# Value projection of the second mixer in products of 512 columns, its weights read twice

## The chip, the cores and the metric

One core of one Trainium2 chip runs the whole program. The metric is the device time of one execution in microseconds (us); the kernel before is given by the median of three runs.

## What is computed

Two transformer blocks on 512 tokens of width 1024, all in float32. The first block mixes by convolutions, attention and pooling and then has a feed-forward part and a gate; the second block has sliding-window attention with sinks and a gated linear attention (GLA), and then a gated feed-forward part with a short convolution. The part around the change is the second block's mixer:

```python
z = h @ w_in[l]
qa, ka, va, qb, kb, vb, rb, gk_lr, ga, gb = split_cols(z)
...
yb = gla_chunked(qb..., kb..., vb.reshape(B, S, H_B, DV_B), gk...)
yb = rmsnorm(yb, gla_norm_g[l]) * jax.nn.silu(rb...)
```

`vb` is 1024 columns wide (4 heads of 256). GLA sums over tokens, so `vb` is wanted with tokens on the partitions, while the other projections are wanted with features on the partitions.

## The kernel before, in words

The 512 tokens are the free dimension of nearly every tensor; features lie on the 128 partitions in 8 tiles of 128. A weight comes as blocks of 128x128; eight blocks, in the order in which they are used, make a **chunk** of 128x1024 (512 KB), and one list, the plan, holds all 1872 blocks (`NBLK`). Each chunk is loaded by a DMA on SP's queue into one of three raw buffers WR, rounded by ACT to its high half WH (`w_hi`, line 2156), and DVE takes WR minus WH as its low half WL (`w_lo`, line 2561). There are four buffers of WH and WL: the high half of a chunk waits until PE has left the chunk four before it (`w_used`), and `ahead` issues it when PE starts a chunk, three chunks ahead; `rest` issues the low half some blocks later, and with it the next load. Activations are split in the same way (AH, AL), and each product is three matmuls: high times high, low times high, high times low.

The order of the work on all five engines comes from one class, `Order`: it writes down steps with `say`, and each engine's program is the same list of steps, of which it runs its own. Between the products of the main line, `tick` is called; side work (a generator that yields how many ticks to wait) puts its next steps there. So a tick is the unit in which side work is spread over the main line, and an engine's instructions stand in the order of the steps: an instruction that waits holds back all behind it on that engine.

The value projection (`values`, `mm_values`, called by `mixer2` after the four `qb` tiles) has the tokens' activations as the stationary operand (128 tokens) and the weights as the moving one. It goes by four quarters `q` of 256 columns; in each by two halves `p` of the tokens (two token tiles of 128); in each over the 8 feature tiles `kt`, with six matmuls of 256 columns and one tick per `kt`. One PSUM bank holds the two token tiles' 256 columns. The half `p` = 1 uses the same weight blocks as `p` = 0, so 64 blocks (8 chunks) serve all. ACT evicts a half bank per token tile (`vb`, line 2465).

Three pieces of side work run between these products:

- `unit2`, the window attention, 16 units: two score products into PSUM (`scores2`, line 2025, P<-KA,QA), a mask and maximum on DVE (`mask2`, lines 3059, 3065, 3067), exponentials on ACT (`exp2`, lines 2388, 2390), a reciprocal on DVE (`scale2`, lines 3073, 3075) and the scaling on ACT (line 2397, SB<-SB,WST), a transpose on PE (`turn2`, line 2033, P<-C,SB), its copy on ACT (line 2406, PT<-P), and the value product (`values2`, line 2046).
- `levels`, the GLA scores by seven levels: differences of the decays (`lv_ref`: DVE line 3087 and POOL line 3501, EX<-BC), their exponential on ACT (`lv_exp`, line 2419, EX<-EX), the scaled queries on DVE (`lv_scale`, lines 3103, 3106, ST<-G,EX) and keys on POOL (line 3522, KT<-G,EX), the **level products** on PE (`lv_mm`, line 2069, P<-ST,KT), and the **puts** of the result on DVE (`lv_put`, lines 3117 to 3119 and 3126, AT<-P). The scaled queries and keys of a level wait for the level products of the level before, and `lv_ref` of the next level waits for the scaled queries and keys of this one.
- the conversions `w_hi` and `w_lo` of the chunks to come.

PSUM banks 0 to 3 are a ring: `ring` takes the closed one that was closed first, `close` gives one back, and the first matmul into a bank waits for its last reader (`free`).

Of the kernel before, what the change touches and what calls it, by code (L numbers as in the profile page):

```python
# [17 lines left out]
CH = 8  # L18
# [4 lines left out]
NBLK = 1872  # L23
# [140 lines left out]
def block(name, r0, c0, nr=128, nc=128):  # L164
    return ((0, 0, name, r0, nr, c0, nc),)
# [31 lines left out]
class Order:  # L197
# [234 lines left out]
    def values(self, q, name, c0):  # L432

        ids = []
        for p in range(2):
            t = self.ring()
            for kt in range(8):
                if p == 0:
                    ids.append(len(self.plan))
                    self.plan.extend(block(name, kt * 128, c0 + 128 * b) for b in range(2))  # L440
                else:
                    for i in (ids[kt], ids[kt] + 1):
                        self.ahead(i)
# [568 lines left out]
    def mixer2(self, post):  # L1012
# [660 lines left out]
def tensor_program(e, w, order, at, m):  # L1673
# [132 lines left out]
    def mm_values(t, p, i, x, kt):  # L1806
        c, wh, wl, ends = weights(i, 2)
# [3 lines left out]
        if kt == 0:  # L1811
            free(t)
        for n in range(2):
            P = m.bank[t.bank][:, 256 * n:256 * n + 256]
            s = slice(256 * p + 128 * n, 256 * p + 128 * n + 128)
            e.matmul(P, xh[:, s], wh, start=kt == 0 and n == 0, stop=False, skip_group_check=True)  # L1816
            e.matmul(P, xl[:, s], wh, start=False, stop=False, skip_group_check=True)  # L1817
            ins = e.matmul(P, xh[:, s], wl, start=False, stop=kt == 7, skip_group_check=True)  # L1818
        if kt == 7:
            ins.then_inc(*at.up("full", "full", t.id))  # L1820
            if ends and p:
                at.also(("full", t.id), "w_used", c)
        elif ends and p:
            ins.then_inc(*at.up("w_used", "w_used", c))
# [265 lines left out]
    def st_mm(n, q, t):  # L2090
        free(t)
        w.wait_ge(*at("st_kd", n))
        w.wait_ge(*at("vb", 3, 3))
# [7 lines left out]
    def gla_out(hh, eh, t):  # L2101
        free(t)
        w.wait_ge(*at("diag_put", 3))
        w.wait_ge(*at("vb", 3, 3))
# [38 lines left out]
def scalar_program(e, w, order, at, m):  # L2143
# [317 lines left out]
    def vb(q, n, t):  # L2461
        if n % 2 == 0:
            w.wait_ge(*at("full", t.id))
        w.wait_ge(*at("roots", "4"))
        e.activation(m.VB[:, n, 256 * q:256 * q + 256], m.bank[t.bank][:, 256 * (n % 2):256 * (n % 2) + 256], ACT.Copy,
                     scale=m.roots("4", 4)[1][:, n:n + 1]).then_inc(*at.up("vb", "vb", q, n))
        if n % 2 == 1:
            at.also(("vb", q, n), "read", t.id)
# [1202 lines left out]
```

## Time and profile before

| | |
|---|---|
| median of 3 runs | 1427.76 us (1426.56 to 1428.2) |
| the profiled execution | 1427.68 us, of which the span from first to last instruction is 1425.9 us |
| PE busy | 1413.9 us, 99% of the span |
| DVE, ACT, POOL busy | 69%, 45%, 15% of the span |
| the value projection, 706.8 to 790.2 us of the span | 83.4 us: PE 82.96, DVE 63.98, ACT 45.98, POOL 29.61 us busy |
| TensorE's granted clock | 0.998 of full speed over the span |

A matmul's duration in the trace includes its way through the array, so matmuls overlap and their durations don't add up to time. The distance from one start to the next does. Times in the text are counted from the start of the span.

### The profile page before, as it was taken

The page shows a single profiled execution, that of the slowest core. Times are in us where ns is not written, and L with a number is a line of the kernel's source. Part 1 is how long each engine was busy: PE and PEld are TensorE (multiplying, and loading weights), DVE is VectorE, ACT ScalarE, POOL GpSimd, SP SyncE. Part 2 cuts the span into 40 slices and gives each one's busy share as a digit, 9 for nine tenths or more (in the row PEclk, how much of TensorE's full clock was granted, in tenths as well). Part 3 has the DMA queues.
Part 4 walks back from the last instruction along what each step waited for, and adds up shares of the span by engine and source line. Part 5 has one row for each costly group of instructions (what it writes and reads, how often), then busy time and mean ns, then how long its engine had stood idle before and what let it go on. Part 6 is the DMA issues. An engine that isn't in the chain of part 4 may idle for free.

```text
span 1425.9 us, 20562 instructions
## 1 busy us (share of the span) xinstructions
PE 1413.9 (99%) x8054; PEld 1213.9 (85%) x8054; DVE 986.4 (69%) x1537; ACT 647.0 (45%) x1028; POOL 214.8 (15%) x136
## 2 busy tenths in 40 slices
PE   9999999999999999999999999999999999999998
PEld 6776798889989888887799888888888889999997
DVE  5777477876676657897696736534452888888877
ACT  5345535534345434545464546323332545455450
POOL 4175224000000011330052104000021000000000
PEclk9999999999999999999999999999999999999999
DMA  6222212333233332222211211323323233333331
GB/s 242 89 75 69 65 60 89 100 97 115 93 100 104 119 104 74 89 67 82 74 60 41 65 45 59 110 90 101 98 90 92 87 105 103 103 93 116 104 106 73
DMA packets 36352, 130.00 MB, mean 91 GB/s; under 512 B 4040, under 2 KB 4296, under 8 KB 36256
## 3 DMA queue, kind: packets, MB, share of 16 engines
q1 hardware_dynamic: 35968, 128.44, 28.5%
q8 instruction: 64, 1.05, 0.3%
q14 instruction: 32, 0.26, 0.1%
q10 hardware_dynamic: 288, 0.26, 0.1%
HBM read 126.56 MB, written 2.10 MB: 90 GB/s over the span
## 4 chain that ended last, share of the span: by engine, by line
PE 91%; DVE 5%; ACT 2%; issue 1%; DMA 1%; ACTq 0%; DVEq 0%; SPq 0%
PE P L1728 17%; PE P L1730 16%; PE P L1729 16%; PE P L1709 5%; PE P L1711 5%; PE P L1710 5%; PE P L1776 4%; PE P L1767 4%; PE P L1769 4%; PE P L2069 2%; DVE WL L2561 1%; PE P L1816 1%; PE P L1817 1%; PE P L1818 1%; PE P L1924 1%
## 5 line engine op out<-in xcount | busy, mean ns | idle before, releaser
L2156 ACT ACTIVATE WH<-WR 128x1024 fp32r<-128x1024 f32 x212 | 223.6, 1055 | 259.2 <-PE P L1730 181.4
L2561 DVE TENSOR_TENSOR WL<-WR,WH 128x1024 fp32r<-128x1024 f32 x196 | 265.5, 1355 | 103.0 <-ACT WH L2156 102.6
L1728 PE MATMUL P<-AH,WH 128*128 128x512 f32 x456 | 186.2, 408 | 0.2 <-DVE BC L3002 0.2
L1730 PE MATMUL P<-AH,WL 128*128 128x512 f32 x456 | 178.2, 391 | 0.0
L1729 PE MATMUL P<-AL,WH 128*128 128x512 f32 x456 | 177.8, 390 | 0.0
L1728 PE MATMUL P<-FH,WH 128*128 128x512 f32 x432 | 168.5, 390 | 0.5 <-issue 0.3
L1729 PE MATMUL P<-FL,WH 128*128 128x512 f32 x432 | 168.4, 390 | 0.0
L1730 PE MATMUL P<-FH,WL 128*128 128x512 f32 x432 | 168.1, 389 | 0.0
L3375 POOL TENSOR_TENSOR AC<-AC,SQ 128x512 f32<-128x512 f32 x27 | 42.5, 1573 | 506.7 <-ACT SQ L2211 505.8
L1709 PE MATMUL P<-AH,WH 128*128 128x256 f32 x400 | 113.5, 284 | 0.3 <-ACT SN L2167 0.2
L1711 PE MATMUL P<-AH,WL 128*128 128x256 f32 x400 | 113.2, 283 | 0.0
L1710 PE MATMUL P<-AL,WH 128*128 128x256 f32 x400 | 113.2, 283 | 0.0
L1728 PEld LDWEIGHTS P<-AH,WH 128*128 128x128 f32 x456 | 85.7, 188 | 21.1 <-issue 4.5
L1730 PEld LDWEIGHTS P<-AH,WL 128*128 128x128 f32 x456 | 85.6, 188 | 18.6
L1729 PEld LDWEIGHTS P<-AL,WH 128*128 128x128 f32 x456 | 85.9, 188 | 16.3 <-issue 0.5
L1767 PE MATMUL P<-AH,WH 128*128 128x512 f32 (+1 forms) x264 | 96.0, 371 | 1.9 <-ACT AH L2202 1.6
L1728 PEld LDWEIGHTS P<-FH,WH 128*128 128x128 f32 x432 | 81.2, 188 | 17.5 <-issue 0.7
L1769 PE MATMUL P<-AH,WL 128*128 128x512 f32 (+1 forms) x264 | 95.2, 367 | 0.8 <-DVE WL L2561 0.5
L1730 PEld LDWEIGHTS P<-FH,WL 128*128 128x128 f32 x432 | 81.1, 188 | 17.1
L1729 PEld LDWEIGHTS P<-FL,WH 128*128 128x128 f32 x432 | 81.2, 188 | 15.8
L1709 PE MATMUL P<-TH,WH 128*128 128x256 f32 x300 | 84.9, 283 | 0.0
L1710 PE MATMUL P<-TL,WH 128*128 128x256 f32 x300 | 84.9, 283 | 0.0
(409 smaller groups left out, 3148.0 us busy)
## 6 DMA issues: line engine op xcount, KB each, us to landing
WR<-in_ws SPq DMA_DIRECT2D x212, 512.0 KB, 3.5
WX<-in_ws SPq DMA_DIRECT2D x21, 512.0 KB, 3.5
out<-Y SPq DMA_DIRECT2D x8, 256.0 KB, 2.0
H<-in_xT SPq DMA_DIRECT2D x3, 512.0 KB, 8.0
C<-in_const SPq DMA_DIRECT2D x1, 946.5 KB, 11.0
H<-in_xT SPq DMA_DIRECT2D x2, 256.0 KB, 4.4
PR<-in_pT SPq DMA_DIRECT2D x1, 512.0 KB, 4.9
WR<-in_ws SPq DMA_DIRECT2D x1, 384.0 KB, 4.8
```

The lines of the kernel that those rows point to most:

```text
L1709: e.matmul(P, wh, xh, start=k in (1, 5, 2) and i == 0, stop=False, skip_group_check=True)
L1710: e.matmul(P, wh, xl, start=False, stop=False, skip_group_check=True)
L1711: ins = e.matmul(P, wl, xh, start=False, stop=k in (2, 3, 4) and i == 3, skip_group_check=True)
L1728: e.matmul(P, wh, xh, start=start, stop=False)
L1729: e.matmul(P, wh, xl, start=False, stop=False)
L1730: ins = e.matmul(P, wl, xh, start=False, stop=stop)
L1767: e.matmul(P, m.WH[:, c % NW, o:o + 128], xh, start=start, stop=False, skip_group_check=True)
L1769: e.matmul(P, m.WL[:, c % NW, o:o + 128], xh, start=False, stop=False, skip_group_check=True)
L1776: ins = e.matmul(m.bank[t.bank][:, cols(a)], wh, m.x(*x)[1][:, cols(a)], start=False, stop=stop, skip_group_check=True)
L2156: e.activation(H, w_source(m, order, k), ACT.Copy).then_inc(*at.up("w_hi", "w_hi", k))
L2561: e.tensor_tensor(L, w_source(m, order, k), H, ALU.subtract).then_inc(*at.up("w_lo", "w_lo", k))
L3375: e.tensor_tensor(AC, AC, m.square(n, i)[:, cols(a)], ALU.add).then_inc(*at.up("summed", "summed", n, i, parts(a)[0]))
```

## The change

The value projection goes by two halves `c` of 512 columns and two halves `p` of the tokens. For each `kt` there are six matmuls of 512 columns, three for each of the two token tiles, and each token tile has a PSUM bank of its own (two banks are open). After each `kt` two ticks follow each other. The weight blocks are put into the plan anew for `p` = 1, so they are loaded and converted twice: 64 blocks more. A `kt` takes four blocks, which must lie in one chunk, so `align` fills the plan up to the next chunk first (7 empty blocks, where before one empty block stood; 6 empty blocks at a later place are no longer needed). ACT evicts a whole bank per token tile.

```diff
-NBLK = 1872
+NBLK = 1936
...
-    def values(self, q, name, c0):
+    def values(self, c, p, name, c0):
 
-        ids = []
-        for p in range(2):
-            t = self.ring()
-            for kt in range(8):
-                if p == 0:
-                    ids.append(len(self.plan))
-                    self.plan.extend(block(name, kt * 128, c0 + 128 * b) for b in range(2))
-                else:
-                    for i in (ids[kt], ids[kt] + 1):
-                        self.ahead(i)
-                self.say("mm_values", t, p, ids[kt], ("A4", kt), kt)
-                self.tick()
-            for n in (2 * p, 2 * p + 1):
-                self.say("vb", q, n, t)
+        ts = [self.ring(), self.ring()]
+        for kt in range(8):
+            i = self.weight([block(name, kt * 128, c0 + 128 * b) for b in range(4)], 4)
+            self.say("mm_values", ts, p, i, ("A4", kt), kt)
+            self.tick()
+            self.tick()
+        for n, t in enumerate(ts):
+            self.say("vb", c, 2 * p + n, t)
             self.close(t)
...
-        assert len(self.plan) % CH not in (0, CH - 1) and len(self.plan) % 2
-        self.plan.append(())
-        for q in range(4):
-            self.values(q, name, at("vb", 256 * q))
+        self.align()
+        for c in range(2):
+            for p in range(2):
+                self.values(c, p, name, at("vb", 512 * c))
...
-        if kt == 0:
-            free(t)
-        for n in range(2):
-            P = m.bank[t.bank][:, 256 * n:256 * n + 256]
+        for n, t in enumerate(ts):
+            if kt == 0:
+                free(t)
+            P = m.bank[t.bank][:]
             s = slice(256 * p + 128 * n, 256 * p + 128 * n + 128)
...
-        e.activation(m.VB[:, n, 256 * q:256 * q + 256], m.bank[t.bank][:, 256 * (n % 2):256 * (n % 2) + 256], ACT.Copy,
+        e.activation(m.VB[:, n, 512 * c:512 * c + 512], m.bank[t.bank][:], ACT.Copy,
```

Since the ticks come in pairs and the conversions twice as often, instructions stand in another order on ACT and DVE. Line numbers of the changed kernel are 6 to 8 lower on these engines (2150 is `w_hi`, 2553 is `w_lo`).

**First place: ACT in the first third of the value projection**, from the exponentials of window unit 2 to the exponential of level 0 (EX<-EX). Before:

```order
L2388 ACTIVATE SB_127,WST<-SB_127,WST 128x256 x2
L2390 ACTIVATE WST<-WST 128x2
L2397 ACTIVATE SB_127<-SB_127,WST 128x256 x2
L2419 ACTIVATE EX<-EX 128x2048
L2465 ACTIVATE VB<-P,NR 128x256 x2
```

The change:

```order
L2382 ACTIVATE SB_127,WST<-SB_127,WST 128x256 x2
L2384 ACTIVATE WST<-WST 128x2
L2150 ACTIVATE WH<-WR 128x1024
L2391 ACTIVATE SB_127<-SB_127,WST 128x256 x2
L2413 ACTIVATE EX<-EX 128x2048
L2150 ACTIVATE WH<-WR 128x1024
```

A high half, which waits until PE has left a chunk, now stands ahead of the scaling and of level 0's exponential.

**Second place: DVE at level 1's products**, from the scaled queries of level 1 (ST<-G,EX) to the first put of its result (AT<-P). Before:

```order
L3067 TENSOR_TENSOR WST<-WST,NR 128x2
L3103 TENSOR_TENSOR ST_117<-G_109,EX 128x16x64
L3087 TENSOR_TENSOR EX<-BC 128x1024
L3117 COPY AT<-P 64x4x64
L3118 COPY AT<-P 32x4x32
```

The change:

```order
L3059 TENSOR_TENSOR WST<-WST,NR 128x2
L2553 TENSOR_TENSOR WL<-WR,WH 128x1024
L3095 TENSOR_TENSOR ST_117<-G_109,EX 128x16x64
L3079 TENSOR_TENSOR EX<-BC 128x1024
L2553 TENSOR_TENSOR WL<-WR,WH 128x1024
L3109 COPY AT<-P 64x4x64
```

A low half now stands ahead of the scaled queries, and another between the differences of level 2 and the puts that give level 1's banks back.

**Third place: DVE from the mask of a window unit to the puts of the next level**, level 4 in the pattern that repeats for the later levels. Before:

```order
L3067 TENSOR_TENSOR WST<-WST,NR 128x2
L3103 TENSOR_TENSOR ST_117<-G_109,EX 128x1024
L2561 TENSOR_TENSOR WL<-WR,WH 128x1024
L3087 TENSOR_TENSOR EX<-BC 128x1024
L3073 TENSOR_SCALAR WST<-WST 128x1 x2
L3075 RECIPROCAL WST<-WST 128x2
L2561 TENSOR_TENSOR WL<-WR,WH 128x1024
L3126 COPY_PREDICATED AT<-C,P 128x64x4 x4
```

The change:

```order
L3059 TENSOR_TENSOR WST<-WST,NR 128x2
L2553 TENSOR_TENSOR WL<-WR,WH 128x1024
L3095 TENSOR_TENSOR ST_117<-G_109,EX 128x1024
L2553 TENSOR_TENSOR WL<-WR,WH 128x1024
L3079 TENSOR_TENSOR EX<-BC 128x1024
L3065 TENSOR_SCALAR WST<-WST 128x1 x2
L3067 RECIPROCAL WST<-WST 128x2
L3118 COPY_PREDICATED AT<-C,P 128x64x4 x4
```

Before, every second level had two low halves and the others none; now each of levels 3 to 6 has two, and the one that stood ahead of the puts stands ahead of the scaled queries.

## Rows read from the trace of the kernel before

**Rows 1.** The page: busy time by engine; chain of waits by engine.

```profile
PE 1413.9 (99%) x8054; PEld 1213.9 (85%) x8054; DVE 986.4 (69%) x1537; ACT 647.0 (45%) x1028; POOL 214.8 (15%) x136
...
PE 91%; DVE 5%; ACT 2%; issue 1%; DMA 1%; ACTq 0%; DVEq 0%; SPq 0%
```

**Rows 2.** Busy time by stretch: us, PE, PEld, DVE, ACT, POOL, PEclk, DMA share, GB/s.

```profile
706.80:790.20 83.40, 82.96 (x694) 76.80 (x693) 63.98 (x122) 45.98 (x96) 29.61 (x11) 1.00 0.15 45
```

**Rows 3.** Groups by line and shape, same stretch: xcount | busy us, mean ns.

```profile
L1816 PE MATMUL P<-WH,AH 128*128 128x256 f32 x128 | 38.9, 304 | 0.0
...
L2561 DVE TENSOR_TENSOR WL<-WR,WH 128x1024 fp32r<-128x1024 f32 x8 | 12.0, 1495 | 0.0
...
L2406 ACT ACTIVATE PT<-P 128x512 f32<-128x512 f32 x6 | 3.6, 597 | 1.4 <-PE P L2033 1.3
```

**Rows 4.** Timeline of PE: start us, us, instruction, [idle before].

```profile
288.46 0.40 PE L1728 MATMUL P<-FH,WH 128*128 128x512 f32 x1
...
299.14 0.39 PE L1730 MATMUL P<-FH,WL 128*128 128x512 f32 x1
...
707.53 0.60 PE L2033 MATMUL P<-C,SB 128*128 128x128 f32 x4
707.88 0.36 PE L1816 MATMUL P<-WH,AH 128*128 128x256 f32 x1
708.09 0.28 PE L1817 MATMUL P<-WH,AL 128*128 128x256 f32 x1
...
708.77 0.70 PE L2025 MATMUL P<-KA,QA 64*128 64x256 f32 x4
...
711.84 0.28 PE L1817 MATMUL P<-WH,AL 128*128 128x256 f32 x1
...
715.20 0.28 PE L1818 MATMUL P<-WL,AH 128*128 128x256 f32 x1
```

**Rows 5.** Timeline of ACT, value projection.

```profile
711.25 1.90 ACT L2419 ACTIVATE EX<-EX 128x2048 f32<-128x2048 f32 x1
...
720.61 1.92 ACT L2419 ACTIVATE EX<-EX 128x2048 f32<-128x2048 f32 x1 [0.43 <-DVE EX L3087]
722.44 0.89 ACT L2397 ACTIVATE SB<-SB,WST 128x256 f32<-128x256 f32 x2
...
763.80 1.90 ACT L2419 ACTIVATE EX<-EX 128x2048 f32<-128x2048 f32 x1
```

**Rows 6.** Timeline of PE, side work in the value projection.

```profile
723.38 0.66 PE L2033 MATMUL P<-C,SB 128*128 128x128 f32 x4 [0.33 <-ACT SB L2397]
...
726.39 2.05 PE L2069 MATMUL P<-ST,KT 128*128 128x128 f32 x16
...
762.12 3.68 PE L2069 MATMUL P<-ST,KT 128*128 128x64 f32 x32
```

**Rows 7.** Timeline of DVE, value projection.

```profile
714.33 3.42 DVE L2561 TENSOR_TENSOR WL<-WR,WH 128x1024 fp32r<-128x1024 f32 x1
...
727.59 0.42 DVE L3117 COPY AT<-P 64x256 f32<-64x256 f32 x1
...
757.32 1.22 DVE L3103 TENSOR_TENSOR ST<-G,EX 128x1024 f32<-128x1024 f32 x1
758.45 1.22 DVE L2561 TENSOR_TENSOR WL<-WR,WH 128x1024 fp32r<-128x1024 f32 x1
759.59 2.92 DVE L3087 TENSOR_TENSOR EX<-BC 128x1024 f32<-128x1024 f32 x1
```

**Rows 8.** Timeline of POOL, value projection.

```profile
713.23 3.44 POOL L3522 TENSOR_TENSOR KT<-G,EX 128x1024 f32<-128x1024 f32 x1 [27.08 <-ACT EX L2419]
...
754.80 2.38 POOL L3522 TENSOR_TENSOR KT<-G,EX 128x1024 f32<-128x1024 f32 x1 [4.03 <-PE P L2069]
...
758.61 2.81 POOL L3501 TENSOR_TENSOR EX<-BC 128x1024 f32<-128x1024 f32 x1 [1.43 <-DVE ST L3103]
...
765.94 2.45 POOL L3522 TENSOR_TENSOR KT<-G,EX 128x1024 f32<-128x1024 f32 x1 [4.52 <-PE P L2069]
```

More of the change, by code:

```diff
@@ L1804, in mm_tokens, with mm_values @@
                 ins.then_inc(*at.up("w_used", "w_used", c))
-    def mm_values(t, p, i, x, kt):
-        c, wh, wl, ends = weights(i, 2)
+    def mm_values(ts, p, i, x, kt):
+        c, wh, wl, ends = weights(i, 4)
         xh, xl = m.x(*x)
@@ L1810, in mm_values @@
         w.wait_ge(*at("x_lo", *x))
-        if kt == 0:
-            free(t)
-        for n in range(2):
-            P = m.bank[t.bank][:, 256 * n:256 * n + 256]
+        for n, t in enumerate(ts):
+            if kt == 0:
+                free(t)
+            P = m.bank[t.bank][:]
             s = slice(256 * p + 128 * n, 256 * p + 128 * n + 128)
-            e.matmul(P, xh[:, s], wh, start=kt == 0 and n == 0, stop=False, skip_group_check=True)
+            e.matmul(P, xh[:, s], wh, start=kt == 0, stop=False, skip_group_check=True)
             e.matmul(P, xl[:, s], wh, start=False, stop=False, skip_group_check=True)
             ins = e.matmul(P, xh[:, s], wl, start=False, stop=kt == 7, skip_group_check=True)
[L1819 to L1824, printed above, removed]
+            if kt == 7:
+                ins.then_inc(*at.up("full", "full", t.id))
+                if ends and n:
+                    at.also(("full", t.id), "w_used", c)
+            elif ends and n:
+                ins.then_inc(*at.up("w_used", "w_used", c))
     def mm_narrow(t, i, kind, M, j):
@@ L2092, in st_mm @@
         w.wait_ge(*at("st_kd", n))
-        w.wait_ge(*at("vb", 3, 3))
+        w.wait_ge(*at("vb", 1, 3))
         for hd in range(2):
@@ L2103, in gla_out @@
         w.wait_ge(*at("diag_put", 3))
-        w.wait_ge(*at("vb", 3, 3))
+        w.wait_ge(*at("vb", 1, 3))
         w.wait_ge(*at("state", 2, 3))
@@ L2459, in gn_out, with vb @@
         e.activation(m.YBH[:, i, :], m.G1[:, i, :], ACT.Copy).then_inc(*at.up("x_hi", "x_hi", "Z2", i))
-    def vb(q, n, t):
-        if n % 2 == 0:
-            w.wait_ge(*at("full", t.id))
+    def vb(c, n, t):
+        w.wait_ge(*at("full", t.id))
         w.wait_ge(*at("roots", "4"))
-        e.activation(m.VB[:, n, 256 * q:256 * q + 256], m.bank[t.bank][:, 256 * (n % 2):256 * (n % 2) + 256], ACT.Copy,
-                     scale=m.roots("4", 4)[1][:, n:n + 1]).then_inc(*at.up("vb", "vb", q, n))
-        if n % 2 == 1:
-            at.also(("vb", q, n), "read", t.id)
+        e.activation(m.VB[:, n, 512 * c:512 * c + 512], m.bank[t.bank][:], ACT.Copy,
+                     scale=m.roots("4", 4)[1][:, n:n + 1]).then_inc(*at.up("vb", "vb", c, n))
+        at.also(("vb", c, n), "read", t.id)
     def rb_silu(i):
```

## The prediction

> **What bounds the kernel now.** I read the page first: PE is busy 99% of the span and 91% of the chain that ended last is PE's [rows 1]. So time is won where PE issues faster and lost where it has to wait. The stage that the change touches is next: in the 83.4 us of the value projection PE is busy 82.96, the granted clock is 1.00, the 2.4 GHz level, the DMA engines are busy 15%, ACT 46 us and DVE 64 us [rows 2]. PE is the limit there too, and DVE is the engine with the least room. The groups of that stage have 384 products of 256 columns, 128 per line; their mean of 304 ns is no cost, because matmuls overlap [rows 3]. The cost is the distance between starts, and the timeline of PE gives it [rows 4]: the 28 distances from 711.84 to 715.20 are 0.120 us each at 256 columns, and the 47 from 288.46 to 299.14 are 0.2272 us each at 512 columns. The last views to read are the timelines of ACT, DVE and POOL in this stage [rows 5, 7, 8], since the change moves their work more than PE's.
>
> **Part 1: products.** 384 x 0.120 = 46.08 us become 192 x 0.2272 = 43.62 us: **-2.5 us**. The moving operand is now the weights instead of activations, of the same type and width, so I take the 512-column row as it stands. The Trainium skill (TensorE: Matmul & The Clock Gate, Back-to-back issue gap) gives N/2.4 + 2.5 ns, 109 ns at 256 columns and 216 ns at 512; by it this part would be worth 384 x 0.109 - 192 x 0.216 = 0.4 us, an estimate from that page. The trace differs at both widths, and its distances decide.
>
> **Part 2: switches.** After side work the first product takes 0.21 us instead of 0.12 (707.88 to 708.09) [rows 4]. In the new order side work interrupts the products 22 times instead of 31, because two ticks fall together. 9 x 0.09 = **-0.8 us**. The side work itself has the same instructions. PE alone would thus win 3.3 us.
>
> **Part 3: what is hidden.** Eight chunks more are loaded: 8 x 512 KB beside a queue that is 15% busy. The added loads wait on the added low halves, and a chunk is still asked for three chunks ahead; a chunk now lasts PE two `kt`, 2.7 us of products and about as much side work, and 3 chunks of that are far more than the conversions need. Cover gone, PE would wait for WL; I see no such wait coming. Eight more high halves on ACT cost about 1 us each, and the evictions get fewer (16 of 256 columns to 8 of 512; the nearest 512-column copy from PSUM is 0.6 us [rows 3]); ACT has 37 us free. In time nothing, but the place in ACT's order counts (part 4). The eight low halves on DVE cost 8 x 1.22 = 9.8 us when alone [rows 7]: DVE goes from 64 to 74 us of a stage of about 80. Nothing on PE as a sum; but see the next three parts.
>
> **Part 4: level 0 starts later.** ACT now has a high half ahead of the scaling of unit 2 and of level 0's exponential. It waits until PE has left the chunk four before, which is the end of the second `kt`: two groups of 6 x 0.227, the switch, and between them a transpose (0.35) and scores (about 0.65) [rows 4], so 3.9 us after the stage's start at 706.8, and about 0.2 us until that is seen. High half 1.06 and scaling 0.9: level 0's exponential starts 6.05 us after the start; before, at 711.25, it was 4.45 [rows 5]. From there the chain is as before: the low half behind it takes 3.42 because POOL's scaled keys hold it (713.23 + 3.44 ends at 716.67, the low half 1.1 us after) [rows 7, 8], then differences, level 1's exponential, and the scaling that ended at 722.44 + 0.89, for which PE's transpose at 723.38 was already idle 0.33 us [rows 5, 6]. PE reaches that place no later than before (17 x 6 x 0.120 = 12.2 us of products, now 9 x 6 x 0.227 = 12.3). So the 1.6 us come through whole: **+1.6 us**.
>
> **Part 5: a bank at level 1.** Level 1 has two sets of products, and the second set takes the banks of the first. PE is back after 16 products (2.0), a value product (0.6) and one `kt` (1.45): 4.0 us after the first set began. On DVE the scaled queries end as that set begins; then differences 1.2, and now a low half, which POOL's own differences hold until 2.9 (2.81 in the row at 758.61 [rows 8]) and which ends at 4.0; three copies, 0.42 the first [rows 7], about 1.05 together, give the first bank back at 5.1. **+1.1 us.** Bounds: 0 (the low half runs before POOL's) and 2.2 (the second bank decides).
>
> **Part 6: levels 3 to 5.** In the level that had two low halves before, POOL's scaled keys began at 754.80 and again at 765.94, 11.14 us apart, both times released by PE's level products [rows 8]: PE set the pace. PE's new pace is 11.14 less 8 ticks' gain (48 x 0.120 - 24 x 0.2272 = 0.3) and a switch: 10.75. The chain beside it is: scaled keys 2.4, a low half 1.2, scaled queries 1.2, then from 758.54 to 762.51 the second low half, POOL's differences and DVE's, which cannot run together, 3.95 [rows 7, 8], reciprocal 0.45, scaling 0.9, exponential 1.9 [rows 5]: 12.0 us. The first low half is new in it; DVE reaches it (four puts, mask) at about the moment when the exponential ends, and whichever of it and POOL's keys is first, the queries come after both. Loss: 1.3 us for each of three levels, less 0.7 us of lead at the first: **+3.2 us**. Bounds: 0 if DVE is through with the low half before the exponential ends (the chain is then 10.8, PE's pace), and 5 if DVE also runs late with the puts, so that a value group waits for its bank. I take the value with the low half in the chain, the order of the program.
>
> **Sum.** -2.5 - 0.8 + 1.6 + 1.1 + 3.2 = +2.6 us on the profiled execution's 1427.68, which lies 0.1 under the median of the runs: **1430.3 us**, 0.18% slower. What the end of the stage loses is not made up later, since PE has no waits there that could shrink. 0.2% (2.86 us) is about what a measurement of this kernel can tell from no change.
>
> **Rivals.**
> (A) Forecast: PE's gain is eaten by the wait for level work, 1430.3 us; parts 5 and 6 at their bounds give 1427.5 to 1433.5.
> (B) The waits don't come: DVE's lead absorbs the low halves. For: PE waits once for 0.33 us in the stage, level products had about 3 us of lead behind the scaled queries (757.32 + 1.22 to 762.12 [rows 6, 7]). Against: that lead is what the chain of part 6 uses up. 1427.7 - 3.3 = 1424.4; with part 4 alone 1426.0.
> (C) Clearly slower: DVE becomes the engine that bounds the stage, because every added low half is caught by a POOL operation, as the one of 3.42 us was. At 1.22 and 1.7 of holding, 8 x 2.9 = 23.4, and 64.0 + 23.4 = 87.4 us, plus about 2 us that DVE must wait for level products: 89.4 against 83.3, 1433.8 us. It decides as soon as DVE's sum is over PE's 80 us, that is if more than half of the added low halves are caught. Against: before, only one of eight took 3.42, their mean is 1.5 [rows 3].
> (D) The wide products don't gain: with a moving operand that also is the weight buffer being refilled, the start distance stays at two of the old ones, 0.240 us. Then part 1 is 0: 1432.8 us. The Trainium skill's rule quoted in part 1 comes near this result by its 0.4 us. Against it: the 0.2272 of row 299.14 was measured while weights were refilled too.
>
> **How the numbers follow.** A 0.55, B 0.24, C 0.16, D 0.05. Faster by more than 0.2% means under 1424.9: half of B, 0.12. Slower means over 1430.6: half of A (0.27), C, and D, 0.48. The same: 0.40. The range leaves out the ends of B and C: 1424.3 to 1434.5. The forecast's own range is 1427.5 to 1433.5.
>
> **What would show it.** Part 1: 192 products whose starts lie 0.227 us apart. Part 2: 22 interruptions with a longer first distance. Part 4: idle time of PE of about 1.9 us at the transpose of unit 3, released by ACT's scaling. Part 5: a wait at level 1's second set, released by DVE's put. Part 6: idle time before the level products of levels 3 to 5, released by DVE's scaled queries, with DVE busy nearly all of the stage. If PE is idle under 1 us in the stage, B holds; if DVE's low halves have a mean near 3 us, C; a distance of 0.240 is D. I would be wrong altogether if PE waited for WH or WL themselves, or if the stages after it changed.

## The result and the profile after

The changed kernel takes 1431.74 us (median of 7 runs, 1430.68 to 1436.07), the kernel before 1427.3 us (7 runs, 1426.52 to 1428.62). The ratio is 1.0035, with a 95% interval of 1.0023 to 1.0047: slower, by more than the 0.2% that the prediction gives as the least that can be told. The loss is 4.4 us, where 2.6 us (1430.3 us) was forecast. The profiled execution took 1436.07 us (span 1434.3), the longest of the seven.

The page of the changed kernel, busy times and the chain that ended last by engine, beside [rows 1]:

```profile
PE 1419.4 (99%) x7862; PEld 1206.0 (84%) x7862; DVE 993.3 (69%) x1545; ACT 649.9 (45%) x1028; POOL 216.1 (15%) x136
...
PE 81%; DVE 11%; ACT 4%; issue 2%; DMA 1%; SPq 0%; DVEq 0%; ACTq 0%
```

PE has 10 points less of the chain, and DVE has 11% instead of 5%. These shares don't measure the loss: a faster version below (the later blocks back in their place) has only 74% for PE. They say who sets the pace. In the value projection, with the chain's pieces there summed by engine, it is DVE's for 48 us and PE's for 19, where it was PE's for 65 and DVE's for 12. What that costs, the busy times of the value projection say. This is the view of windows (us, then busy time and count of PE, PEld, DVE, ACT, POOL; granted clock; DMA share; GB/s), to be read beside [rows 2]:

```profile
707.60:793.60 86.00, 82.82 (x502) 64.84 (x501) 80.61 (x136) 51.69 (x97) 31.25 (x11) 1.00 0.32 99
```

PE is busy as long as before (82.82 against 82.96 us) and idle about 3 us instead of 0.4. DVE is busy 80.6 of 86.0 us instead of 64.0 of 83.4. From the first value product to the first product behind the stage it is 85.94 us against 83.30: +2.6. PE's longest waits there, in the view of waits (engine, line, what it waited for: us in total, times, longest):

```profile
PE P L2027 <- ACT SB L2391: 1.7, 1, 1.7
PE P L2063 <- DVE AT L3111: 0.8, 1, 0.8
PE P L2040 <- ACT PT L2400: 0.3, 1, 0.3
```

Three places stand behind that in PE's timeline: two transposes with the scores behind them, the transpose of unit 3, and the second set of level 1.

```profile
716.76 0.38 PE L2027 MATMUL P<-C,SB 128*128 128x128 f32 x2
717.08 0.49 PE L2019 MATMUL P<-KA,QA 64*128 64x128 f32 x4
717.50 0.50 PE L1810 MATMUL P<-WH,AH 128*128 128x512 f32 x1
717.84 0.40 PE L1811 MATMUL P<-WH,AL 128*128 128x512 f32 x1
718.07 0.39 PE L1812 MATMUL P<-WL,AH 128*128 128x512 f32 x1
...
725.78 0.66 PE L2027 MATMUL P<-C,SB 128*128 128x128 f32 x4 [1.69 <-ACT SB L2391]
...
733.80 0.38 PE L2063 MATMUL P<-ST,KT 128*128 128x128 f32 x1 [0.82 <-DVE AT L3111]
```

The products stand 0.23 us apart, the first after side work 0.34 (717.50 to 717.84). Transposes and scores now follow each other with no product between them.

Outside the stage there is one more loss. In the last feed-forward part the first pair of products by seven (from its first product to the next P<-FH,WH) takes 11.63 us instead of 10.40. Twelve products ahead of its end PE waits, in its timeline:

```profile
1187.30 0.39 PE L1703 MATMUL P<-AH,WH 128*128 128x256 f32 x1 [1.16 <-ACT SN L2161]
```

ACT's timeline shows where ACT is late ahead of SN:

```profile
1170.53 1.04 ACT L2150 ACTIVATE WH<-WS 128x1024 fp32r<-128x1024 f32 x1
1172.23 0.63 ACT L2498 ACTIVATE SS<-SS 128x512 f32<-128x512 f32 x1 [0.66 <-DVE SS L3266]
...
1185.92 1.06 ACT L2150 ACTIVATE WH<-WS 128x1024 fp32r<-128x1024 f32 x1 [2.73 <-DVE WS L2573]
1186.89 0.36 ACT L2161 ACTIVATE SN<-P 128x256 f32<-128x256 f32 x1
```

The pair's first high half (WH<-WS) stands ahead of the silu of the short convolution (SS<-SS). In the kernel before, the silu is first (1163.56) and the high half behind it (1164.10), and the same product at 1179.17 is 0.35 us behind the one ahead of it, with no idle time shown. The link between silu and SN is only followed in part: the high half at 1185.92 waits for DVE, and DVE for a load (WX<-in_ws) until 1184.40, 7.2 us behind the pair's first product; in the kernel before it is 6.0 us (1176.27). The experiments below show that the place of the blocks makes the loss. The blocks behind the value projection start at plan place 1056, a multiple of eight, where they started at 986: they lie two places earlier in their chunks, so the conversions are asked for at other steps.

Last, the profile of the changed kernel has a stretch of 6.83 us at a granted clock of 0.5 (the 1.2 GHz level) from about 876 us on. Products of 512 columns stand 0.43 us apart there instead of 0.23, so it costs about 3.2 us, and it isn't in the profile before. Is it part of the loss? The experiments ask that too.

### The profile page after: what moved, and what is told of

It is laid out like the page before. It is cut to its first block, busy times and chain, and to the rows that moved or that the text cites. A ratio compares the mean times of both kernels' runs of the same rounds, so it can differ in the third digit from the quotient of the medians.

```text
span 1434.3 us, 20168 instructions
## 1 busy us (share of the span) xinstructions
PE 1419.4 (99%) x7862; PEld 1206.0 (84%) x7862; DVE 993.3 (69%) x1545; ACT 649.9 (45%) x1028; POOL 216.1 (15%) x136
## 4 chain that ended last, share of the span: by engine, by line
PE 81%; DVE 11%; ACT 4%; issue 2%; DMA 1%; SPq 0%; DVEq 0%; ACTq 0%
PE P L1722 15%; PE P L1724 15%; PE P L1723 15%; PE P L1703 5%; PE P L1705 5%; PE P L1704 5%; PE P L1770 4%; PE P L1761 4%; PE P L1763 4%; DVE WL L2553 2%; ACT WH L2150 1%; DVE EX L3079 1%; DMA WR<-in_ws 1%; DVE ST L3095 1%; PE P L1918 1%
## 5 line engine op out<-in xcount | busy, mean ns | idle before, releaser
L2553 DVE TENSOR_TENSOR WL<-WR,WH 128x1024 fp32r<-128x1024 f32 x204 | 268.7, 1318 | 125.9 <-ACT WH L2150 125.7
L2150 ACT ACTIVATE WH<-WR 128x1024 fp32r<-128x1024 f32 x220 | 231.5, 1053 | 205.9 <-PE P L1724 133.1
```

The source lines that it names most:

```text
L2150: e.activation(H, w_source(m, order, k), ACT.Copy).then_inc(*at.up("w_hi", "w_hi", k))
L2553: e.tensor_tensor(L, w_source(m, order, k), H, ALU.subtract).then_inc(*at.up("w_lo", "w_lo", k))
```

## The experiments

Theory at the start: wide products gain less than forecast, doubled conversions make the waits of the stage, and the place in the chunk makes the loss at the pair. Rivals: ticks in pairs make the waits; the raw buffers' turn makes the loss at the pair; the clock makes the loss. "Stage" is the length of the value projection, from its first product to the first product behind it; "pair" is the pair of products by seven. Before: 83.30 and 10.40 us; the change: 85.94 and 11.63.

**The later blocks back in their place.** Two empty blocks behind the value projection:

```diff
-NBLK = 1936
+NBLK = 1944
...
                 self.values(c, p, name, at("vb", 512 * c))
+        self.plan.extend(((), ()))
```

> The changed kernel with two empty blocks behind the value projection, so that the later blocks stand in their chunks as they did before the change (the feed-forward part then again fills six empty blocks ahead of its first pair of products by seven). Theory: of the 4.4 us, 2.5 to 2.7 are lost in the value projection and 1.9 at that first pair, near 1165 to 1180 us, where conversions now meet the convolution's side work in another order. Expected: the value projection as in the changed kernel (85.7 us), the distance from its end to the end of the program again that of the kernel before, the whole 1.9 us faster than the changed kernel, a ratio near 1.0018 to before. Rival: the loss at the pair is an accident of one execution (or of the granted clock): then the ratio stays at 1.0035.

Stage 85.90, pair 10.47; 1430.89 us, ratio 1.0028 (1.0016 to 1.0039). The pair is back, and that is 1.2 us of the trace (0.9 in the medians), not the 1.9 expected; the medians alone couldn't tell it, since the two intervals overlap. The silu stands ahead of the high half again.

**Conversions once, products wide.** The second half of the tokens uses the first half's blocks:

```diff
-NBLK = 1936
+NBLK = 1872
...
-            i = self.weight([block(name, kt * 128, c0 + 128 * b) for b in range(4)], 4)
+            i = i0 + 4 * kt
+            if p == 0:
+                self.plan.extend(block(name, kt * 128, c0 + 128 * b) for b in range(4))
+            if kt < 2 if p == 0 else kt > 1:
+                self.ahead(i)
...
+            i0 = len(self.plan)
             for p in range(2):
-                self.values(c, p, name, at("vb", 512 * c))
+                self.values(c, p, name, at("vb", 512 * c), i0)
...
-                if ends and n:
+                if ends and n and p:
...
-            elif ends and n:
+            elif ends and n and p:
```

> Products of 512 columns, but each weight converted once: the four chunks of a half stay in their buffers for both halves of the tokens. Theory (the doubled conversions make the stage's waits): with 8 instead of 16 chunks converted the wait at unit 3 falls to about 0.5 us and the others to under 0.5 together, the stage takes about 82.5 us; at the first pair of the feed-forward part the 1.9 us stay, since the blocks stand in their chunks as in the changed kernel, though the count of chunks, and so the raw buffers' turn, is that of the kernel before. Ratio 1.0008. Rivals: if the raw buffers' turn makes the loss at the pair, it vanishes here (ratio 0.9995); if the pairing of ticks makes the stage's waits, the stage stays near 85 us.

Stage 81.71, pair 11.61; 1429.24 us, ratio 1.0011 (1.0002 to 1.002). The wide products without a second conversion (ticks in pairs and the filled-up chunk included) make the stage 1.6 us shorter than before; converting twice costs 4.2 us. The pair is late here too, though no chunk was added: it isn't the raw buffers' turn.

**Conversions twice, products of 256 columns**, the kernel before otherwise:

```diff
-NBLK = 1872
+NBLK = 1936
...
-                if p == 0:
-                    ids.append(len(self.plan))
-                    self.plan.extend(block(name, kt * 128, c0 + 128 * b) for b in range(2))
-                else:
-                    for i in (ids[kt], ids[kt] + 1):
-                        self.ahead(i)
-                self.say("mm_values", t, p, ids[kt], ("A4", kt), kt)
+                i = self.weight([block(name, kt * 128, c0 + 128 * b) for b in range(2)], 2)
+                self.say("mm_values", t, p, i, ("A4", kt), kt)
...
-            if ends and p:
+            if ends:
...
-        elif ends and p:
+        elif ends:
```

> The kernel before with its products of 256 columns, one tick each, but its weights loaded and converted twice: the other half of the change alone. The count of chunks is the changed kernel's, the blocks' place in the chunks is that of the kernel before. Theory: the added conversions cost through their place in the order; the stage goes from 83.2 to about 85 us (waits at unit 3 and at level 1), and nothing is lost at the first pair; ratio 1.0013. Rivals: if the pairing of ticks made the waits, the stage stays at 83.2 (ratio 1.000); if the turn of the raw buffers makes the loss at the pair, 1.9 us are lost there too (ratio 1.0026).

Stage 87.24, more than the 85 expected, pair 10.44; 1431.98 us, ratio 1.0029 (1.0018 to 1.0041). The timeline of PE has the wait without any wide product or pair of ticks:

```profile
725.93 0.66 PE L2027 MATMUL P<-C,SB 128*128 128x128 f32 x4 [2.84 <-ACT SB L2391]
```

So the doubled conversions make it. A part of the 87.24, about 1.5 us, is a stretch at the 1.2 GHz level that begins 1.4 us behind the end of this wait. The turn of the raw buffers is the changed kernel's, the place in the chunk the old one, and the pair is not late: the place decides.

**Conversions asked for behind the two ticks**, so that level 0's work stands ahead of them:

```diff
-            i = self.weight([block(name, kt * 128, c0 + 128 * b) for b in range(4)], 4)
+            i = len(self.plan)
+            self.plan.extend(block(name, kt * 128, c0 + 128 * b) for b in range(4))
             self.say("mm_values", ts, p, i, ("A4", kt), kt)
             self.tick()
             self.tick()
+            self.ahead(i)
```

> The changed kernel with each chunk's conversions asked for behind the two ticks of a feature tile instead of ahead of its products; same instructions, so the high halves stand behind the scaling of unit 3 and the exponentials, the low halves behind the puts. Theory (place in the order costs, not the work): the idle times of PE in the value projection (1.8 us at the transpose of unit 3, 1.0 at level 1's second set, about 1 at later levels) vanish but for some 0.5 us; the stage takes 82.4 us instead of 85.7, the whole 3.3 us less than the changed kernel, a ratio of 1.0012. Rival (the work itself costs: DVE and POOL hold each other): the waits move to other places and the stage stays over 85 us, ratio 1.0035.

A miss. 1437.07 us, ratio 1.0063 (1.005 to 1.0075), stage 86.84. Level 1's wait is gone (others of 0.2 to 0.6 us are in its place), but that of unit 3 is as long as it was, since a high half now stands ahead of unit 2's exponentials on ACT (709.54) instead of behind them. Level 0's exponential starts 6.1 us after the stage's start as before. PE's timeline also shows the clock:

```profile
725.27 0.65 PE L2029 MATMUL P<-C,SB 128*128 128x128 f32 x4 [1.74 <-ACT SB L2393]
725.85 0.93 PE L2021 MATMUL P<-KA,QA 64*128 64x256 f32 x4
726.71 0.79 PE L1812 MATMUL P<-WH,AH 128*128 128x512 f32 x1
727.30 0.63 PE L1813 MATMUL P<-WH,AL 128*128 128x512 f32 x1
727.73 0.63 PE L1814 MATMUL P<-WL,AH 128*128 128x512 f32 x1
```

Behind 1.74 us of waiting and the small products of unit 3, the products stand 0.43 us apart, 0.23 at the 2.4 GHz level, for 3.41 us: 3.41 x (1 - 0.23/0.43) = 1.6 us. That is a small part of the 9.5 us that this version loses; why its other runs take more than the profiled one (1434.62, the fastest of five) stays open.

**The changed kernel a second time.**

> The changed kernel itself, a second time. In its first profile a stretch of 6.83 us at the lower clock level (1.2 GHz) lay 83 us behind the value projection and cost about 3.3 us. Theory one: the loss against the kernel before sits in the value projection (about 2.6 us longer) and at the first pair of products by seven in the last feed-forward part (11.6 us instead of 10.4), and that stretch is an accident of one execution. Then the value projection takes 85.9 us again (85.6 to 86.2), the way from its end to the first product of the last feed-forward part 368.9 us instead of 372.0, the pair 11.6, and the ratio to the kernel before is 1.003 (1.002 to 1.004). Rival: the stretch belongs to the changed kernel and carries the loss. Then it is there again at the same place, with 372 us, and the ratio without it would be about 1.001.

Stage 85.93, pair 11.79; 1431.85 us (11 runs), ratio 1.0034 (1.0024 to 1.0043). From the stage's end to the last feed-forward part 370.47 us, so the clock fell here too, at the same place, for 3.41 us instead of 6.83. PE's timeline of this run:

```profile
872.62 0.95 PE L2116 MATMUL P<-C,BC 128*128 128x1 f32 x8
873.43 1.03 PE L2116 MATMUL P<-C,SQ 128*128 128x1 f32 x8
874.32 1.22 PE L2116 MATMUL P<-C,VB 128*128 128x1 f32 x8
875.41 0.78 PE L1722 MATMUL P<-AH,WH 128*128 128x512 f32 x1
875.98 0.63 PE L1723 MATMUL P<-AL,WH 128*128 128x512 f32 x1
```

It falls behind 24 products of one column, which take 2.8 us. Both answers were half right: the stretch is no accident of one execution, but it doesn't carry the loss. The version above with the old place has no such stretch in its profile, and that execution took 1430.60 us, 2.9 more than the profiled one before. And in the runs with a mean granted clock of 1.000 the changed kernel takes 1430.68 to 1431.45 us (five runs), the kernel before 1426.22 to 1427.05 (six).

**One tick behind each token tile**, instead of two behind both:

```diff
-            self.say("mm_values", ts, p, i, ("A4", kt), kt)
-            self.tick()
-            self.tick()
+            for n in range(2):
+                self.say("mm_values", ts, p, i, ("A4", kt), kt, n)
+                self.tick()
...
-    def mm_values(ts, p, i, x, kt):
+    def mm_values(ts, p, i, x, kt, half):
...
-        for n, t in enumerate(ts):
+        for n, t in ((half, ts[half]),):
```

> The changed kernel with one tick behind each token tile's three products of 512 columns, instead of two ticks behind both tiles' six. Conversions are still made twice. Theory one: the doubled conversions make the waits, and two ticks in a row only cost switching: eight transposes are directly followed by score products, 0.17 us more each (1.4 us), against nine interruptions saved at about 0.1 us each (0.9). So the waits stay (about 4 us of PE in the stage, the one at the transpose of window unit 3 among them), and the value projection takes 85.4 us (84.9 to 86.0), ratio 1.003 (1.002 to 1.0038). Rival: ticks in pairs make the waits, because they put two units' or levels' steps on PE ahead of the engines that feed them. Then the waits fall under 1.5 us, the stage takes about 83 us, and the ratio is 1.0015 or less.

Worse than both expected: stage 87.41, 1434.65 us, ratio 1.0046 (1.0032 to 1.006). The waits grow. At unit 3 PE comes to the transpose 0.7 us sooner than in the changed kernel, and ACT is 0.8 later: the added high half ahead of level 0's exponential waits for PE to leave a chunk, and more side work now stands ahead of that. PE's timeline:

```profile
725.22 0.66 PE L2027 MATMUL P<-C,SB 128*128 128x128 f32 x4 [3.23 <-ACT SB L2391]
```

**Conversions once, old place** (the first two edits together, `NBLK` 1880):

> The changed kernel with the second half of the tokens using the weights that the first half used (loaded and converted once), and with two empty blocks behind the value projection, so that all later blocks have the place in their chunks that they had in the kernel before. Theory one, from single parts: the products of 512 columns with conversions made once give a value projection of 81.7 us against 83.3 before, and the place in the chunk gives the pair of products by seven its 10.4 us back. So the value projection takes 81.7 us (81.4 to 82.0), the pair 10.45, and the kernel 1426.3 us, ratio 0.9990 (0.9984 to 1.0000), where the version without the empty blocks had 1.0011. Rival: the pair depends on which raw buffer and which load comes when and not on the place in the chunk alone, so that it stays at 11.6 us and the ratio stays at 1.0011 (1.0005 to 1.0017).

Stage 81.73, pair 10.56; 1427.27 us (11 runs), ratio 0.9998 (0.999 to 1.0007). The pair came back, against the rival. Its window and PE's only wait in the stage, by the views of windows and waits:

```profile
706.70:788.55 81.85, 81.41 (x503) 65.17 (x502) 57.92 (x128) 44.72 (x89) 31.90 (x11) 1.00 0.17 52
...
PE P L2033 <- ACT SB L2397: 0.4, 1, 0.4
```

**The same with one tick behind each token tile:**

> The version with conversions once and the later blocks in their old place, with one tick behind each token tile's three products. Theory one: transposes are followed by products of 512 columns again (eight at 0.17 us, 1.4 us won), nine more interruptions cost 0.9 us, no new wait: value projection 81.2 us (80.7 to 81.7), ratio 0.9987 (0.998 to 0.9998). Rival: the interruptions cost as much as they win, because the slow first distance behind side work is about 0.33 us at 512 columns against 0.23, and the products behind it are slower too: 82.0 us or more, ratio 0.9995 or more.

Stage 82.40; 1429.83 us, ratio 1.0012 (1.0003 to 1.0021): the rival. Its times by the kind of instruction from which a distance between PE's starts is counted (each cell is a sum of such distances over the stage, in us; a wait of PE counts to the instruction ahead of it):

| from | before | wide, once | wide, once, one tick | changed kernel |
|---|---|---|---|---|
| value products | 50.75 | 47.75 | 49.92 | 51.52 |
| transposes | 2.46 | 3.84 | 2.45 | 3.84 |
| scores, window values | 8.94 | 8.94 | 8.95 | 8.94 |
| level products | 21.14 | 21.20 | 21.09 | 21.64 |
| stage | 83.30 | 81.73 | 82.40 | 85.94 |

Eight transposes with scores right behind them stand 0.20 us ahead of these, and only 0.03 ahead of a product, so pairs of ticks cost 1.4 us. One tick at a time wins them back, and nine more interruptions take 1.45 us again. And the wait at unit 3 grows by 0.7 (0.60 to 1.32 us above the usual distance).

**Which conversion?** In three versions the added chunks' conversions are 8 columns wide. What stays in the buffer is the half of the chunk four before it, and that is the same weights, so nothing is left out of the result (the words on other data in the expectations don't hold). First the low halves alone:

```diff
-            e.tensor_tensor(L, w_source(m, order, k), H, ALU.subtract).then_inc(*at.up("w_lo", "w_lo", k))
+            s = slice(0, 8 if c in (120, 121, 122, 123, 128, 129, 130, 131) else 1024)
+            e.tensor_tensor(L[:, s], w_source(m, order, k)[:, s], H[:, s], ALU.subtract).then_inc(
+                *at.up("w_lo", "w_lo", k))
```

> The changed kernel, with the low halves of the eight added chunks made of 8 columns instead of 1024; the rest of those low halves keeps what an earlier chunk left, so the products of the second half of the tokens are computed from other data. All loads, high halves and the order on every engine stay. Theory one: DVE's added low halves make most of the waits of the value projection (the one of 3.4 us behind level 0's scaled queries, the one that holds the bank at level 1's second set, those of the later levels). Level 0's exponential still starts 6.1 us after the stage's start; from there to level 1's exponential 8.6 us instead of 9.3, so the wait at the transpose of unit 3 falls from 1.84 to about 1.1, and the other waits (about 1.6 together) go: value projection 83.3 us (82.8 to 83.9), ratio 1.0017 (1.0008 to 1.0025). Rival: ACT's added high halves make them, by what they hold back; then the stage stays over 85 us and the ratio over 1.0025.

Stage 82.51, lower than expected; 1430.17 us, ratio 1.0016 (1.0007 to 1.0025). All waits but one are gone, in the views of windows and waits:

```profile
705.85:788.40 82.55, 81.64 (x502) 65.11 (x501) 64.77 (x136) 52.32 (x97) 32.80 (x11) 1.00 0.33 103
...
PE P L2027 <- ACT SB L2391: 0.9, 1, 0.9
```

Then the high halves alone, by the same edit of `w_hi` (`H[:, s]` and the source `[:, s]`):

> The changed kernel, with the high halves of the eight added chunks made of 8 columns instead of 1024 (the rest keeps an earlier chunk's values, so the second half of the tokens is computed from other data). All loads, low halves and the order stay; a narrow high half still waits until PE has left its buffer. Theory one: the high halves count for little: in the version with conversions once, level 0's exponential starts 5.6 us after the stage's start without any high half ahead of it, because unit 2's exponentials come later in the new order; so here it is 5.6 instead of 6.1, the wait at the transpose of unit 3 falls by 0.5 to about 1.3, the other waits stay: value projection 85.3 us (84.8 to 85.8), ratio 1.003 (1.002 to 1.004). Rival: the high halves make most of it (the step of my forecast that put 1.6 us on the high half ahead of level 0's exponential): exponential at 4.5 us, wait 0.5 or less, stage 84.2 us or less.

Stage 85.12; 1433.17 us, ratio 1.0035 (1.0022 to 1.0047). ACT's timeline has level 0's exponential 5.59 us after the stage's start at 706.76, and PE's the wait at unit 3:

```profile
712.35 1.90 ACT L2414 ACTIVATE EX<-EX 128x2048 f32<-128x2048 f32 x1
...
724.47 0.33 PE L2027 MATMUL P<-C,SB 128*128 128x128 f32 x1 [1.23 <-ACT SB L2392]
```

Then both:

> The changed kernel, with high and low halves of the eight added chunks made of 8 columns (what is left out as in the two versions before). The loads, their queue and the order stay. Theory one: the time of the conversions is what costs, and neither the eight loads nor the waits for a buffer: value projection 82.0 us (81.6 to 82.5), close to the 81.7 of the version that converts once, ratio 1.0008 (1.0000 to 1.0016), the rest being the pair of products by seven at 11.6 us. Rival: the wait for PE's release of a buffer, which a narrow high half keeps, or the loads, cost by themselves: 83 us or more.

Stage 82.05; 1430.57 us, ratio 1.0021 (1.0012 to 1.003). The stage is as expected: eight more loads (DMA share 0.33 in the profile with narrow low halves) and the waits for a buffer cost 0.3 us at most. The ratio is above what was expected; this profile has a stretch of 3.41 us at the lower level at the place of the 24 one-column products. Of the 4.2 us, the low halves make 3.1 to 3.4 (85.12 less 82.05; 85.94 less 82.51), the high halves 0.5 to 0.8 (82.51 less 82.05; 85.94 less 85.12), both together 3.9. The 0.3 that is left lies in level 1's second set of products, where a narrow low half, held by POOL, still stands ahead of the puts (1.86 us).

**Conversions once, old place, a second time:**

> The version with products of 512 columns, conversions once and the later blocks in their old place, a second time, to narrow its interval beside 0.9998 (0.9990 to 1.0007). Its profile was 1.3 us shorter than the profile of the kernel before (82 against 83 us in the value projection). Theory one: that gain is real: ratio 0.9993 (0.9985 to 1.0001), value projection 81.7 us again. Rival: it is no more than the spread of single runs: ratio 1.0000 or more.

1428.38 us, ratio 1.0004 (0.9995 to 1.0013). Its profile is of an execution of 3606.58 us, so its stage isn't read. With 0.9998 above: no difference from the kernel before that these runs can tell, though the profile above was 1.3 us shorter; so the 1.6 us of the stage aren't shown as time won by the whole kernel. In 7 of its 21 runs the mean granted clock was 0.996, in 3 of the 53 of the kernel before beside them. But that doesn't hide a gain: at a mean clock of 0.998 its seven runs have a median of 1427.7 us, those of the kernel before 1427.2. Where the other executions lose those 1.3 us stays open.

## Why the prediction was right, and where only its sum was

The direction, the likeliest case (A) and the stage's +2.6 us came true. That the stage's sum came out is luck in part: forecast were -3.3 and +5.9, found -1.6 and +4.2. The whole kernel lost 4.4 us, 1.8 more than forecast. The forecast itself lay just under the 1430.6 us from which it counted as slower (0.48 for slower, 0.40 for the same). Its own range of 1427.5 to 1433.5 doesn't follow from its parts: with parts 5 and 6 at their bounds the sum gives 1426.0 to 1433.2.

- **Part 1 and Part 2: a term was missing.** Products and switches together gained 50.75 - 47.75 = 3.0 us in the version without doubled conversions, against 3.3 forecast, but not as forecast: products with a product on either side stand 0.231 us apart on average, not 0.2272, which makes part 1 worth 1.5 us instead of 2.5; part 2 is worth the other 1.5 instead of 0.8, since not only the first product behind side work is slow but also the last one ahead of it (0.21 us to the side work before, 0.12 undisturbed). What failed besides is "The side work itself has the same instructions": it has, but they stand behind each other otherwise, and transposes with scores behind them cost 1.4 us. PE alone thus won 1.6, not 3.3. Rival D is out: these distances are 0.231 us, not 0.240. The 0.4 us by the Trainium skill (TensorE: Matmul & The Clock Gate, Back-to-back issue gap, which gives this formula for an isolated product) is not what the runs show either.
- **Part 3: right in the stage.** No product there waits for WH or WL, and loads cost nothing that can be seen. It overlooked the blocks behind: at the pair's first product PE does wait 0.16 us for WL (1177.20), the sign that the prediction had named for being wrong, though it is small.
- **Part 4: the size was right, the reason mostly not.** Level 0's exponential was to start 6.05 us after the stage's start; it started 6.06 us after it. ACT's timeline of the changed kernel:

```profile
711.90 1.06 ACT L2150 ACTIVATE WH<-WR 128x1024 fp32r<-128x1024 f32 x1 [0.62 <-PE P L1812]
712.87 0.89 ACT L2391 ACTIVATE SB<-SB,WST 128x256 f32<-128x256 f32 x2
713.67 1.90 ACT L2413 ACTIVATE EX<-EX 128x2048 f32<-128x2048 f32 x1
```

  The wait at unit 3 grew from 0.49 to 1.84 us above the usual distance, 1.35 against 1.6: ACT's scaling came 1.6 later, and PE came to the place 0.25 later, not "no later than before". But of the 1.6 us the high half ahead of the exponential makes only 0.5: without it (narrow, or in the versions that convert once) it starts after 5.59 us. The rest is a later reciprocal of unit 2 (4.57 us after the stage's start, 3.42 before): its exponentials end 0.65 us later, behind a transpose that stands behind six wide products, and two chunks are converted at the start of the stage now, so that DVE, busy with the second low half, comes to the reciprocal another 0.5 later. DVE's timeline of the version that converts once, in the old place:

```profile
709.85 1.22 DVE L2559 TENSOR_TENSOR WL<-WR,WH 128x1024 fp32r<-128x1024 f32 x1
710.98 0.33 DVE L3071 TENSOR_SCALAR WST<-WST 128x1 f32<-128x1 f32 x2
711.35 0.17 DVE L3073 RECIPROCAL WST<-WST 128x2 f32<-128x2 f32 x1
```

  In the kernel before, the reciprocal is at 710.24. (The expectation of the narrow high halves gave unit 2's exponentials as the reason; the number held, the reason is half of it.) That lateness alone costs little: without added conversions the wait is 0.60. Each conversion has its part: 1.07 without low halves, 1.38 without high halves, 0.61 without both.
- **Part 5: right.** The second set of level 1 stands 1.21 us behind the product ahead of it, 1.0 more than usual, released by DVE's put; 1.1 was forecast. The low half ahead of that put took 2.92 us, held by POOL's differences (2.93 us from 728.76) as the step had it. Within the set, waits for the other banks' puts cost 0.3 more. DVE's timeline of the changed kernel:

```profile
729.85 2.92 DVE L2553 TENSOR_TENSOR WL<-WR,WH 128x1024 fp32r<-128x1024 f32 x1
...
733.45 0.30 DVE L3111 COPY AT<-P 32x128 f32<-32x128 f32 x1
```

- **Part 6: right for DVE, wrong for PE.** 3.2 us were forecast, as waits of the level products of levels 3 to 5 for DVE's scaled queries. None of these came. In PE's timeline of the changed kernel the products of levels 3, 4 and 5 each start at the usual 0.23 us behind the product ahead, with no idle time:

```profile
755.17 3.68 PE L2063 MATMUL P<-ST,KT 128*128 128x64 f32 x32
...
766.14 3.68 PE L2063 MATMUL P<-ST,KT 128*128 128x64 f32 x32
...
777.85 3.68 PE L2063 MATMUL P<-ST,KT 128*128 128x64 f32 x32
```

  Against the version that converts once, 1.4 us of the 4.2 are lost from level 2 on, in five places of 0.2 to 0.4 us: level 2's products, which do wait for the scaled queries (743.32), two value groups that start late in a new bank (748.64, released by DVE's put, and 771.20), as the prediction had it for its upper bound, and two value products of the window attention that wait for ACT's copy (753.07, 775.76). The same waits stand in the second profile of the changed kernel. What did come is the slowing of DVE. DVE's and POOL's timelines of the changed kernel show the chain:

```profile
744.32 2.92 DVE L3079 TENSOR_TENSOR EX<-BC 128x1024 f32<-128x1024 f32 x1
...
750.13 1.23 DVE L2553 TENSOR_TENSOR WL<-WR,WH 128x1024 fp32r<-128x1024 f32 x1
751.27 3.40 DVE L3095 TENSOR_TENSOR ST<-G,EX 128x1024 f32<-128x1024 f32 x1
754.60 1.21 DVE L2553 TENSOR_TENSOR WL<-WR,WH 128x1024 fp32r<-128x1024 f32 x1
755.73 2.91 DVE L3079 TENSOR_TENSOR EX<-BC 128x1024 f32<-128x1024 f32 x1
```

```profile
750.51 3.07 POOL L3514 TENSOR_TENSOR KT<-G,EX 128x1024 f32<-128x1024 f32 x1 [4.36 <-ACT EX L2413]
754.75 2.81 POOL L3493 TENSOR_TENSOR EX<-BC 128x1024 f32<-128x1024 f32 x1 [1.16 <-DVE ST L3095]
```

The first low half (750.13) keeps DVE busy when the exponential ends, POOL's keys begin first, and the queries behind both take 3.40 us instead of 1.22 [rows 7]. From one level's differences to the next it is 11.41 us (744.32 to 755.73), against 12.0 in the sum. The other side was off as well: PE's own pace, in the version without added conversions, was 11.1 us per level (750.6 to 772.8 for two) instead of 10.75, for the reasons that stand under Part 2. So a level was to lose 0.3 us by this sum, not 1.3, and the lead of the scaled queries over the level products took even that.
- **Rival B** is out (idle time about 3 us). **Rival C** had the right engine and the wrong way: DVE is at 94% of the stage, the chain is DVE's for 48 of 86 us, and its added low halves make most of the loss, but 15 of 17 low halves took 1.22 us and two 3.40 and 2.92, where C had all the added ones caught. What is caught is the scaled queries behind them: 3.4 us in four of seven.
- **A sentence that failed: "or if the stages after it changed".** One did: the pair lost 1.2 us, by place in the chunk. This is most of the 1.8 us that the kernel lost beyond the forecast; the other 0.6 isn't placed. The change's `align` and the six empty blocks no longer needed stood in the diff and the plan; the step that was left out is to follow the blocks behind an edit to the next point where they are aligned.

## What to carry to other kernels

An engine with room on average can be the one that delays: price added work on it by what stands behind it in its queue, here queries that a low half of 1.2 us made 2.2 us longer. Savings on the engine that bounds are worth nothing ahead of a place that another chain sets: with conversions once and one tick behind each token tile PE came to unit 3 0.7 us sooner and waited 0.7 us longer. And where a plan packs blocks into chunks, an edit moves everything behind it up to the next alignment; pad it back, and measure the edit and the shift apart.

## What the runs showed of the hardware

A DVE instruction of few columns with two operands in SBUF was held by a POOL instruction as long as one of 1024 columns, 2.2 us (3.40 instead of 1.22 above). In the version with narrow low halves, by DVE's timeline, a low half of 8 columns took 0.17 us alone and 2.34 us beside POOL's keys; the queries ahead of it, which began 0.04 us before the keys, took 1.23:

```profile
755.98 0.17 DVE L2554 TENSOR_TENSOR WL<-WR,WH 128x8 fp32r<-128x8 f32 x1
756.43 1.23 DVE L3097 TENSOR_TENSOR ST<-G,EX 128x1024 f32<-128x1024 f32 x1 [0.28 <-ACT EX L2413]
757.57 2.34 DVE L2554 TENSOR_TENSOR WL<-WR,WH 128x8 fp32r<-128x8 f32 x1
```

POOL's timeline beside it:

```profile
756.47 3.42 POOL L3516 TENSOR_TENSOR KT<-G,EX 128x1024 f32<-128x1024 f32 x1 [4.35 <-ACT EX L2413]
```

In these rows the one that begins first runs at its own speed, and the other one waits for its end. The Trainium skill (SBUF — State Buffer, Who interferes with whom) says that the two engines' shared ports are locked for a whole instruction by the one that comes first; the rows agree.

Score products right behind transposes stand 0.20 us behind the last of these, value products 0.03. And the granted clock fell to the 1.2 GHz level for 3.41 or 6.83 us at places where PE had waited 1.7 to 2.8 us, or had run 24 products of one column; in other executions it didn't fall at the same places (waits of 1.69 and 3.23 us above). What decides isn't shown.
